# One more even/odd step in the transforms of a long convolution, inside a full encoder layer

## The reference

```python
def bidirectional_fftconv(u, h_fwd, h_bwd):
    """y[t] = sum_{s<=t} h_fwd[t-s] u[s] + sum_{s>t} h_bwd[s-t] u[s]; u (B,L,C)."""
    L = u.shape[1]
    n = 2 * L
    kern = jnp.concatenate([h_fwd, jnp.zeros((1, h_fwd.shape[1]), F32), h_bwd[1:][::-1]], axis=0)
    uf = jnp.fft.rfft(u.astype(F32), n=n, axis=1)
    kf = jnp.fft.rfft(kern, n=n, axis=0)
    y = jnp.fft.irfft(uf * kf[None], n=n, axis=1)[:, :L]

# in hyena(): x0, x1, v are short convolutions of the projection (512 channels each)
    v = v * x1
    v = bidirectional_fftconv(v, h_fwd, h_bwd) + v * filt_bias
    y = v * x0      # then an RMSNorm in 8 groups of 64 channels
```

## Time and profile before

| | |
|---|---|
| median of 3 runs | 1014.75 us (1013.47 to 1020.14) |
| profiled execution | 1013.12 us, its span from first to last instruction 1010.9 us |
| PE busy | 1002.7 us, 99% |
| PE weight loads | 806.6 us, 80% |
| DVE busy | 533.9 us, 53% |
| ACT busy | 332.7 us, 33% |
| chain that ended last | PE 97%, DVE 2%, issue 1% |

### The profile page before, as it was taken

The page is one execution under the profiler, slowest core; times in us unless marked ns, Lnnn a source line. Parts: engine busy times, 40 slices in busy tenths (PEclk is TensorE's granted clock), DMA queues, the critical chain, the costliest instruction groups (busy, mean ns, idle before and its releaser), DMA issues.

```text
span 1010.9 us, 12095 instructions
## 1 busy us (share of the span) xinstructions
PE 1002.7 (99%) x4556; PEld 806.6 (80%) x4556; DVE 533.9 (53%) x748; ACT 332.7 (33%) x487; POOL 38.3 (4%) x42
## 2 busy tenths in 40 slices
PE   9999999999999999999999999999999999999997
PEld 8887888888777887676777878788888888888887
DVE  6645444444344538658887755744544544433333
ACT  6322223222222232233544453432322322322221
POOL 0000000000010110000000002200000000001100
PEclk9999999999999999999999999999999999999999
DMA  8432322223333336121221222222232232333322
GB/s 284 149 105 83 105 87 100 98 93 97 94 94 99 94 117 239 56 84 42 81 81 42 92 97 84 88 100 94 92 104 89 98 103 87 95 94 98 96 73 84
DMA packets 35474, 100.92 MB, mean 100 GB/s; under 512 B 3878, under 2 KB 12455, under 8 KB 35181
## 3 DMA queue, kind: packets, MB, share of 16 engines
q1 hardware_dynamic: 34940, 98.51, 30.0%
q0 software_dynamic: 352, 1.85, 0.5%
q10 hardware_dynamic: 144, 0.05, 0.0%
HBM read 96.19 MB, written 4.21 MB: 99 GB/s over the span
## 4 chain that ended last, share of the span: by engine, by line
PE 97%; DVE 2%; issue 1%; ACT 0%; ACTq 0%; POOL 0%; DVEq 0%; POOLq 0%
PE bank L1487 27%; PE bank L1489 27%; PE bank L1488 27%; PE bank L1774 1%; PE bank L1717 1%; PE bank L1871 1%; PE bank L1873 1%; PE bank L1748 1%; PE bank L1872 1%; PE bank L1757 1%; PE bank L1690 1%; PE bank L1551 1%; PE bank L1552 1%; PE bank L1553 1%; DVE x_lo L907 1%
## 5 line engine op out<-in xcount | busy, mean ns | idle before, releaser
L1487 PE MATMUL bank<-x_hi,w_hi 128*128 128x512 f32 x864 | 340.7, 394 | 0.6 <-DVE w_lo L847 0.6
L1489 PE MATMUL bank<-x_hi,w_lo 128*128 128x512 f32 x864 | 336.4, 389 | 0.0
L1488 PE MATMUL bank<-x_lo,w_hi 128*128 128x512 f32 x864 | 336.3, 389 | 0.0
L847 DVE TENSOR_TENSOR w_lo<-raw,w_hi 128x1024 fp32r<-128x1024 f32 (+1 forms) x162 | 196.2, 1211 | 197.8 <-ACT w_hi L469 193.2
L469 ACT CAST w_hi<-raw 128x1024 fp32r<-128x1024 f32 (+1 forms) x162 | 166.2, 1026 | 188.5 <-PE bank L1489 177.5
L1487 PEld LDWEIGHTS bank<-x_hi,w_hi 128*128 128x128 f32 x864 | 162.2, 188 | 40.5 <-issue 7.3
L1489 PEld LDWEIGHTS bank<-x_hi,w_lo 128*128 128x128 f32 x864 | 162.2, 188 | 34.3
L1488 PEld LDWEIGHTS bank<-x_lo,w_hi 128*128 128x128 f32 x864 | 162.3, 188 | 33.0 <-issue 0.7
L1487 PE MATMUL bank<-h_hi,w_hi 128*128 128x512 f32 x330 | 128.8, 390 | 0.0
L1489 PE MATMUL bank<-h_hi,w_lo 128*128 128x512 f32 x330 | 128.4, 389 | 0.0
L1488 PE MATMUL bank<-h_lo,w_hi 128*128 128x512 f32 x330 | 128.4, 389 | 0.0
(11 more groups left out here) (261 smaller groups left out, 787.1 us busy)
## 6 DMA issues: line engine op xcount, KB each, us to landing
raw<-in_ffn_w_gate SPq DMA_DIRECT2D x43, 512.0 KB, 3.3
raw<-in_ffn_w_up SPq DMA_DIRECT2D x43, 512.0 KB, 3.3
raw<-in_ffn_w_down SPq DMA_DIRECT2D x32, 512.0 KB, 3.5
raw<-in_w_in SPq DMA_DIRECT2D x24, 512.0 KB, 3.3
raw<-in_ffn_w_down SPq DMA_DIRECT2D x16, 384.0 KB, 3.1
raw<-in_w_out SPq DMA_DIRECT2D x8, 512.0 KB, 4.0
resid<-in_x_t SPq DMA_DIRECT2D x8, 256.0 KB, 4.6
resid_dram<-resid SPq DMA_DIRECT2D x1, 2048.0 KB, 12.4
```

Of the source, the lines that this page charges most:

```text
L847: nc.vector.tensor_tensor(w_lo[:, half, 0:kb, :], raw[:, slot, 0:kb, :], w_hi[:, half, 0:kb, :].bitcast(F32), ALU.subtract).then_inc(w_spl ...
L1487: nc.tensor.matmul(dst, w_hi[:, half, k, :], hi, start=first and k == 0, stop=False)
L1488: nc.tensor.matmul(dst, w_hi[:, half, k, :], lo, start=False, stop=False)
L1489: ins = nc.tensor.matmul(dst, w_lo[:, half, k, :], hi, start=False, stop=last and k == kb - 1)
```

## The change

Values and filter are transformed with one more even/odd step, and the steps of the product are put later.

- Frequencies are counted so that block 1 is block 0 mirrored (`odd` in `constants`). The even positions' sums are then wanted for block 0 only: a sum over positions divisible by four and one over the other even positions are each made once, and their sum and difference give both blocks.
- For the filter: `kernel_sums(0)` and `kernel_sums(2)` make two even sums (banks 4 and 6) and the odd sum, four matmuls; `kernel_sums(1)` and `kernel_sums(3)` the odd sum of block 1 only, two matmuls. ACT copies one even bank for cosines and one for sines. DVE gets `kernel_parities(c)`, two operations of 128 x 512, in iterations 4 and 5. `filters(t)` reads its columns of `act3` with a step of 4 for t = 0 and 1, and a step of 2 for t = 2 and 3.
- For the values: `forward_evens` after block 9 has four matmuls over 64 rows, in two pairs, and one of a single row; `forward_odds(0)` and `forward_odds(1)` after block 10 have two full matmuls each. DVE gets `value_parities(c)`, two operations each, where `cosines(0)` and `sines(0)` were, and these follow with those of block 1 after block 10. `vx` is written in an order of which `turn_values` reads contiguous columns; before, it read every second column.
- DVE's order in heads 0 to 2 puts each step of the product later; the last, `imaginary_parities(1)`, is now after `split_qk(3, 1)`.
- The four forward tables are loaded with 3 of 4 blocks each.

```diff
@@ ACT
             def kernel_even(k):
-                act.wait_ge(kern_sum, k + 1)
-                nc.scalar.copy(ksig[:, k, :], bank[4 + 2 * (k % 2)][:]).then_inc(kern_even, 1)
+                act.wait_ge(kern_sum, 2 * k + 1)
+                nc.scalar.copy(ksig[:, 2 * k + 1, :], bank[6][:]).then_inc(kern_even, 1)
-            def forward_even(f):
...
+            def forward_even(k):
+
+                act.wait_ge(dft_even, k + 1)
+                nc.scalar.copy(sig1[:, k, :], bank[5 + 2 * k][:]).then_inc(spec_even, 1)
-                for k in ((), (), (), (), (0, 1), (2,), (3,), ())[n]:
+                for k in ((), (), (), (), (0,), (1,), (), ())[n]:
                     kernel_even(k)
...
             forward_even(0)
+            forward_even(1)
...
             exps(0, 0)
             split(8, N_MIX + 12)
-            forward_even(1)
@@ DVE
-                    back_from = lambda at: bass.AP(z.tensor, z.offset + at, [z.ap[0], [-1, FQ]])
-                    nc.vector.tensor_tensor(vx[:, g, 0:FQ], z[:, 1 + FQ:1 + S], back_from(1 + FQ), ALU.add)
-                    nc.vector.tensor_tensor(vx[:, g, FQ:S], back_from(1 + S), z[:, 1:1 + FQ], ALU.subtract).then_inc(vx_set, 1)
+                    count = lambda at, way: bass.AP(z.tensor, z.offset + at, [z.ap[0], [4 * way, FQ // 4], [2 * way, 2], [way, 2]])
+                    near, far = (vx[:, g, u * P:(u + 2) * P + P].rearrange("p (v x j m) -> p v m j x", v=1, x=3, j=2)[:, 0, :, :, 0::2] for u in range(2))
+                    nc.vector.tensor_tensor(near, count(1 + FQ, 1), count(1 + FQ, -1), ALU.add)
+                    nc.vector.tensor_tensor(far, count(1 + S, -1), count(1, 1), ALU.subtract).then_inc(vx_set, 1)
+            def kernel_parities(c):
+
+                dve.wait_ge(kern_even, c + 1)
+                even, twice = bank[4][:], ksig[:, 2 * c + 1, :]
+                nc.vector.tensor_tensor(ksig[:, 2 * c, :], even, twice, ALU.add)
+                x, y = (twice, even) if c else (even, twice)
+                nc.vector.tensor_tensor(twice, x, y, ALU.subtract).then_inc(kern_evens, 1)
+                dve.wait_ge(kern_evens, c + 1)
             def kernel_spectrum(k):
-                dve.wait_ge(kern_even, k + 1)
+                dve.wait_ge(kern_sum, k + 1)
...
+            def value_parities(c):
+
+                dve.wait_ge(spec_even, c + 1)
+                even, twice = bank[4 + 2 * c][:], sig1[:, c, :]
+                nc.vector.tensor_tensor(sig0[:, c, :], even, twice, ALU.add)
+                x, y = (twice, even) if c else (even, twice)
+                nc.vector.tensor_tensor(twice, x, y, ALU.subtract).then_inc(evens_set, 1)
+                dve.wait_ge(evens_set, c + 1)
...
                 taps(n)
+                if n in (4, 5):
+                    kernel_parities(n - 4)
...
             split_qk(0, 0)
             split_qk(0, 1)
-            cosines(0)
-            sines(0)
+            value_parities(0)
+            value_parities(1)
...
             split(8, N_MIX + 12)
-            cross_near(0)
-            cross_far(0)
+            cosines(0)
+            sines(0)
             cosines(1)
             sines(1)
             logits(0, 1)
-            own_near(0)
             combine(0, 1)
...
             combine(0, 2)
-            own_far(0)
+            cross_near(0)
             logits(0, 3)
             project(12)
-            imaginary(0)
             combine(0, 3)
+            cross_far(0)
...
             logits(1, 1)
+            real(0)
             split(8, N_MIX + 16)
             combine(1, 1)
-            cross_near(1)
+            real_parities(0)
             project(15)
...
             logits(2, 3)
             project(20)
+            real_parities(1)
             combine(2, 3)
             split(8, N_MIX + 22)
             project(21)
             split_qk(3, 0)
             split_qk(3, 1)
+            imaginary_parities(1)
             split(8, N_MIX + 23)
@@ PE
+            def of_order(t):
+
+                return (slice(0, 4 * P - 3, 4), slice(2, 4 * P - 1, 4), slice(1, 2 * P, 2), slice(2 * P + 1, 4 * P, 2))[t]
...
-                    nc.tensor.matmul(bank[4 + 2 * (t % 2) + k][:], act3[half, of_parity(t)], w4[half, :], start=True, stop=True).then_inc(filt_sum, 1)
+                    nc.tensor.matmul(bank[4 + 2 * (t % 2) + k][:], act3[half, of_order(t)], w4[half, :], start=True, stop=True).then_inc(filt_sum, 1)
...
-                for t in range(NT):
-                    ins = nc.tensor.matmul(bank[4 + 2 * f + t // 2][:], table[:, t, f * P:(f + 1) * P], filt[:, t, :],
-                                           start=t % 2 == 0, stop=t % 2 == 1)
-                ins.then_inc(kern_sum, 1)
+                if f == 0:
+                    nc.tensor.matmul(bank[4][:], table[:, 0, :], filt[:, 0, :], start=True, stop=True)
+                    nc.tensor.matmul(bank[6][:], table[:, 1, :], filt[:, 1, :], start=True, stop=True)
+                nc.tensor.matmul(bank[5 + 2 * f][:], table[:, 2 + 2 * f, :], filt[:, 2, :], start=True, stop=False)
+                nc.tensor.matmul(bank[5 + 2 * f][:], table[:, 3 + 2 * f, :], filt[:, 3, :], start=False, stop=True).then_inc(kern_sum, 1)
...
-            def forward(f):
...
+            def forward_evens():
                 pe.wait_ge(vx_nat_set, NG)
-                wait(pe, spec_read, f)
...
+                low, high = slice(0, P // 2), slice(P // 2, P)
+                nc.tensor.matmul(bank[4][:], cos_u[low, 0, :], vx_nat[low, 0, :], start=True, stop=False)
+                nc.tensor.matmul(bank[5][:], cos_u[high, 0, :], vx_nat[high, 0, :], start=True, stop=True)
+                nc.tensor.matmul(bank[4][:], end_u[:], vx_nat[0:1, 1, :], start=False, stop=True).then_inc(dft_even, 1)
+                nc.tensor.matmul(bank[6][:], sin_u[low, 0, :], vx_nat[low, 1, :], start=True, stop=True)
+                nc.tensor.matmul(bank[7][:], sin_u[high, 0, :], vx_nat[high, 1, :], start=True, stop=True).then_inc(dft_even, 1)
+
+            def forward_odds(f):
+
+                pe.wait_ge(evens_set, f + 1)
+                nc.tensor.matmul(bank[4 + 2 * f][:], cos_u[:, 1 + f, :], vx_nat[:, 2, :], start=True, stop=True).then_inc(dft_sum, 1)
+                nc.tensor.matmul(bank[5 + 2 * f][:], sin_u[:, 1 + f, :], vx_nat[:, 3, :], start=True, stop=True).then_inc(dft_sum, 1)
...
             project(9)
-            forward(0)
+            forward_evens()
 
             pe.wait_ge(qk_split, 2)
             scores(0, 0)
             project(10)
-            forward(1)
+            forward_odds(0)
+            forward_odds(1)
             scores(0, 1)
```

More of the change, by code:

```diff
@@ L61 @@
 FQ = S // 2
-FORWARD_BANKS = (4, 5, 6, 7)
 INV_BANKS = (4, 5, 1, 4)
@@ L125, in build @@
         k_hi, k_hi_at = place("k_hi", [P, S], F32R)
[L127 to L130 removed]
+        cos_t, cos_t_at = place("cos_t", [P, 8, P])
+        sin_t, _ = place("sin_t", [P, 8, P])
+        cos_u, cos_u_at = place("cos_u", [P, 4, P])
+        sin_u, _ = place("sin_u", [P, 4, P])
         cos_i, _ = place("cos_i", [P, 2, FQ + 1])
@@ L172, in build @@
         bias_row, _ = place("bias_row", [1, D_HY], at=att_o_at + 8 * S)
-        end_u, _ = place("end_u", [1, FQ], at=att_o_at + 12 * S)
+        end_u, _ = place("end_u", [1, P], at=att_o_at + 12 * S)
         ksig, _ = place("ksig", [P, 4, S], at=attn_t_at)
@@ L249, in build @@
         kern_even, kern_sum, kern_set = sem("kern_even"), sem("kern_sum"), sem("kern_set")
-        dft_sum, spec_even, spec_read, spec_set = (sem(n) for n in ("dft_sum", "spec_even", "spec_read", "spec_set"))
+        dft_even, dft_sum, spec_even, evens_set, spec_read, spec_set, kern_evens = (
+            sem(n) for n in ("dft_even", "dft_sum", "spec_even", "evens_set", "spec_read", "spec_set", "kern_evens"))
         ends_zero, long_odd, long_sum, long_half, long_read, hy_o_set = (
@@ L656, in attended @@
                 nc.scalar.copy(att_o[:, h, :], bank[6][:]).then_inc(att_o_set, 1)
-            def forward_even(f):
-                if f:
-                    act.wait_ge(dft_sum, 8)
-                for k in range(2):
-                    act.wait_ge(dft_sum, 4 * f + 2 * k + 1)
-                    nc.scalar.copy((sig0, sig1)[f][:, 2 * k, :], bank[FORWARD_BANKS[2 * k]][:]).then_inc(spec_even, 1)
+            def forward_even(k):
+                act.wait_ge(dft_even, k + 1)
+                nc.scalar.copy(sig1[:, k, :], bank[5 + 2 * k][:]).then_inc(spec_even, 1)
             def long_sines(g):
@@ L1346, in _ @@
             split_qk(1, 1)
-            real(0)
+            own_near(0)
             split(8, N_MIX + 15)
             logits(1, 0)
-            real_parities(0)
+            own_far(0)
             combine(1, 0)
-            imaginary_parities(0)
+            imaginary(0)
             project(14)
             logits(1, 1)
+            real(0)
             split(8, N_MIX + 16)
             combine(1, 1)
-            cross_near(1)
+            real_parities(0)
             project(15)
@@ L1363, in _ @@
```

(33 more changed lines are left out.)

39 lines of the change are left out of this document (13 added, 26 removed).

## The result

| | before | changed |
|---|---|---|
| median of 4 runs beside each other | 1014.72 us (1013.47 to 1020.14) | 1007.80 us (1007.58 to 1009.55) |
| ratio of the times | | 0.994, 95% interval 0.9919 to 0.9961 |
| profiled execution, and its span | 1013.12, 1010.9 us | 1007.62, 1005.4 us |

One run of the kernel before took 1020.14 us, so medians are compared. The profiled executions differ by 5.50 us, where the forecast's sum was 5.8.

A forecast was written before the change was run, and what follows sets the result against it. PE's own instructions were taken to bound the kernel. Savings of 3.42 + 0.95 + 1.25 + 0.2 = 5.8 us from 1014.0 gave 1008.2 us, 0.6% faster; range 1006.6 to 1009.7, with rivals 1005.0 to 1012.5.

The forecast's parts named there:

- What bounds the kernel: Whole kernel: PE's own instructions in order set the time; PE busy 1002.7 of 1010.9 us, waits 3.1 us.
- Part 1: Filter's kernel_sums: four matmuls of 0.86 go, saving 3.42 us; DVE's four new operations lie in its idle time.
- Part 2: Values' even sums after block 9: 0.95 us saved, not 1.6, since scores(0, 0) then wait 0.65 for k's low part.
- Part 3: Values' odd sums after block 10: four full matmuls and one mode change, 3.52 against 4.77, saving 1.25 us.
- Part 4: Changed steps of access: vx's transposes load without a step, saving 0.2 us of at most 1.1; filters and folds cost nothing.
- the prediction's own sign of being wrong: Anywhere: new PE waits above 1 us elsewhere, pairs' starts that do not coincide, or a fold above 0.5 us.
- Part 5: Product put later on DVE in heads 0 to 2: nothing lost, slack of 0.4 us left at attend_turns(2).
- Base: Whole kernel: 1014.0 us, the middle of the undisturbed executions, as the time from which the saving is taken.
- Pairs in series: Rival at forward_evens: the 64-row pairs don't overlap, even sums give nothing or -0.1, time 1009.2 us; chance 0.08.
- Strided accesses: Rival at folds and filters: folds take four times 0.42, PE waits at turn_values(3), time 1009.8 us; chance 0.08.
- More than the sum: Rival: transposes give their full 1.1 and the k chain ends 0.65 earlier, sum 7.3, time 1006.7 us; chance 0.09.
- DVE as the bound: Rival at attend_turns(2): DVE's added work comes to light, PE waits 6.4 us, time 1014.6 us; chance 0.03.

The follow-up runs named there:

- full_row_evens: The changed kernel with the four 64-row matmuls of forward_evens run over all 128 rows, so they can't pair: 1009.35 us, ratio 0.9955 to the kernel before.
- order_only: The kernel before with only the spectral product's steps put later on DVE: 1013.51 us, ratio 0.9992 to the kernel before.
- product_late: The changed kernel with real_parities(1) done a second time ahead of combine(2, 3): 1009.88 us, ratio 0.9963 to the kernel before.
- k_split_first: The changed kernel with DVE making the low parts of q and k before that of block 11's weights: 1007.44 us, ratio 0.9938 to the kernel before.

## Why the forecast held, step by step

- **What bounds the kernel.** "Microseconds of PE work that go away are saved, unless PE then arrives before its inputs": shown. PE's busy time fell by 6.1, the span by 5.5.
- **Part 1, 3.42.** Measured 3.36, alone and together: 0.84 for each matmul and not 0.86. DVE's four operations lay in its idle time: its wait before block 5's read-out is 1.63 now, 3.55 in the earlier trace rows, and the loss of 1.9 is what the earlier block and the new work take from it. DVE's timeline:

```profile
417.33 0.69 DVE L1079 TENSOR_TENSOR zpad<-bank,rinv 128x512 f32<-128x512 f32 x1 [1.63 <-PE bank L1507]
```

- **Part 2, 0.95.** Measured 0.95 (1.04 less 0.09). The chain through k's split was unchanged, as said, and it ended last. The wait reads 0.48 and not 0.65, because the forecast counted from start to start and the row counts from the end of the record before, 0.16 later. Both are the same gap. What was missing is 0.11 for the first matmul behind it.
- **Part 3, 1.25.** Measured 1.25; forward_odds to scores takes 3.52, as said.
- **Part 4.** The transposes gave the 0.20 that was taken, not the 1.1 of all loads. full_row_evens shows it by itself: without the change of mode the values' first sum comes 7.20 behind turn_values, where the kernel before has 7.40. So most of the 69 ns off each load was time that PE did not wait for. The folds are the step that failed, and the prediction's own sign of being wrong, a fold above 0.5, came up: 0.62 to 0.64. They were costed at nothing because the *last* fold has cover, and that was right at turn_values. But those of taps(1) stand on DVE ahead of its read-out of filters(1), which PE's filters(3) need, and DVE had 0.05 to spare there. The forecast looked at one of four places. filters' loads, at nothing with a bound of 0.2, cost 0.13 alone. Both together cost 0.20, not 0.35. The sum was 0.26 too high, 0.20 of it here and the other 0.06 in part 1.
- **The rule of the Trainium skill** (page "SBUF — State Buffer", the note on cachelines in the section "Door 1: The DMA port swizzle", by which an access that moves to a new 16-byte line each time pays) fits the accesses with a step of 4 or more: loads of act3 306 ns against 186 without a step, folds 0.62 against 0.42. At a step of 2 a line still holds two of the values, and there the traces disagree: act3 192 against 186, next to nothing, but vx 209 against 140. Why the loads of vx gained is not shown. The rival built on it, folds four times as long and 1.6 us lost, was far too dear; a fold became half as long again.
- **Part 5, nothing.** Shown by order_only alone (+0.02) and by product_late: the room at attend_turns(2) was 0.34, against the 0.4 forecast. DVE's load through heads 0 to 2 rose less than forecast, from 76.18 to 77.23 of 90 us (86%, not 88%); between the same two landmarks, the first odd sum and attend_turns(2), it rose by 0.4 us and not by 2.8:

```profile
460.00:550.00 90.00, 90.00 (x429) 65.86 (x426) 77.23 (x155) 43.28 (x83) 1.61 (x3) 1.00 0.20 69
```

- **Base.** The sum was set against the middle of the undisturbed executions, 1014.0, and not the low profiled one. The median came out at 1007.80, 0.4 below 1008.2. That closeness is partly luck: the later series put the kernel before at 1013.5 to 1013.6, so the base was 0.4 to 0.5 too high for them, the sum was 0.3 too large, and the changed kernel itself gave 1008.63 when it ran again. Over all runs the medians of the spans differ by 5.8, the times' by 4.8 and 6.9 in the two series that ran the changed kernel.
- **Rivals.** Pairs in series: refuted by the starts 0.01 apart and by full_row_evens. Strided accesses: mechanism there, price wrong. More than the sum: refuted at the transposes; its second half, the k chain earlier by the wait, does not happen by itself, but k_split_first brings it about. DVE as the bound: refuted for this kernel. But the point from which it would decide was wrong: the forecast named the end of DVE's 13.8 us of idle time, and product_late made PE wait with 12.5 us of idle time left. It decides from 0.34 us at attend_turns(2).

## What to carry to other kernels

Two small costs that meet at one wait don't add: repaired alone, each gives back little or nothing (0 and 0.06 here), and only both repairs together pay (0.21). A wait in a row is not yet a cost: ask how much later the other arm ends (here 0.49 waited, 0.05 to spare). When an operation that is repeated gets slower, look at every place where it stands and not at the last: the cost comes where some engine already waits. And once an edit shortens PE's work so that a wait appears, look first at the other engine's order; here 0.73 of 0.97 us came from moving a split of weights that nobody needed yet.

## What the runs showed of the hardware

- **A wait costs PE more than its figure.** A wait of 0.48 cost 0.73, one of 0.83 cost 1.05: 0.2 to 0.25 on top. 0.16 of it is in how the rows are drawn (a record ends 0.16 after the next one could start: 0.59 against 0.43, 0.39 against 0.23), and at the scores 0.11 more went with the first matmul behind the pause.
- **The price of a weight load goes by its step, but not evenly.** Loads of 64 rows by 128 columns of fp32: 186 ns side by side, 192 with a step of 2, 306 with a step of 4. Loads of 128 by 128: 140 and, with a step of 2, 209.
- **Start to start, a step costs in both directions**: 0.34 for a plain fold of 256 elements (392.72 to 393.06), 0.45 with scattered writes, 0.56 with reads at a step of 4.
- **The granted clock can fall in the mixing step.** The profiled execution of order_only has a span of 1018.9 where the other ten of its runs have 1010.9 to 1011.9. Windows of it (length, busy time and count of PE, PEld, DVE, ACT, POOL, then PEclk, DMA share, GB/s):

```profile
570.00:575.00 5.00, 4.22 (x28) 3.75 (x28) 4.86 (x11) 1.00 (x2) 0.00 (x0) 0.84 0.00 0
575.00:580.00 5.00, 5.00 (x22) 4.05 (x22) 4.52 (x15) 2.92 (x8) 0.00 (x0) 0.50 0.61 200
585.00:590.00 5.00, 5.00 (x17) 4.23 (x16) 0.00 (x0) 0.00 (x0) 0.00 (x0) 0.50 0.50 161
590.00:595.00 5.00, 5.00 (x36) 4.40 (x36) 1.94 (x6) 2.66 (x7) 0.00 (x0) 0.96 0.00 0
```

and PE's timeline inside:

```profile
580.83 0.63 PE L1488 MATMUL bank<-x_lo,w_hi 128*128 128x512 f32 x1
581.25 0.63 PE L1489 MATMUL bank<-x_hi,w_lo 128*128 128x512 f32 x1
```

From about 574 to 590 us PE ran at the lower of its two levels, 1.2 GHz, with matmuls 0.43 apart and not 0.23. Ahead of the fall stand inverse's matmuls of 128 columns and a stretch in which PE was idle 0.78 of 5 us. From 575 on PE was busy without a gap, and the clock rose near 590. That cost about 8 us (1018.9 less the 1010.9 of the fastest run), which is more than the whole change. The kernel before does the same work there at 1.00 in its own trace, with PE idle for 0.81 of 5 us in the same window, so that idle time alone did not bring the fall about. Its cause is open. It lies behind inverse(0), so no distance in the table holds it.
